# Two hi/lo pairs of matmul operands moved to other SBUF offsets in a float32r transformer kernel

## The reference

```python
def rms_norm(x, g):
    y = x * lax.rsqrt(jnp.mean(x * x, axis=-1, keepdims=True) + EPS)
    return y * g

def swiglu(h, w_gate_up, w_down):
    gate, up = jnp.split(h @ w_gate_up, 2, axis=-1)
    return (jax.nn.silu(gate) * up) @ w_down

# first block, layer i of 4
x = x + mixer_i(rms_norm(x, norm_mix_g[i]))
x = x + swiglu(rms_norm(x, norm_ffn_g[i]), ffn_w_gate_up[i], ffn_w_down[i])
# second block, layer i of 2
h = h + 0.5 * swiglu_ffn(rmsnorm(h, norm_ffn1[i]), w_ffn1_in[i], w_ffn1_out[i])
u = rmsnorm(h, norm_mix[i]) @ w_mix_in[i]
h = h + concat([ssd(u), attention(u)]) @ w_mix_out[i]
h = h + 0.5 * swiglu_ffn(rmsnorm(h, norm_ffn2[i]), w_ffn2_in[i], w_ffn2_out[i])
```

## Time and profile before

| | |
|---|---|
| median of 3 runs | 2777.88 us (2777.1 to 2781.78) |
| profiled execution | 2778.99 us |
| its span | 2777.2 us |
| mean granted TensorE clock | 0.973 of full |
| TensorE matmul busy | 2613.1 us, 94% |
| VectorE busy | 1834.5 us, 66% |
| ScalarE busy | 1266.6 us, 46% |
| moved by DMA | 433.01 MB, mean 156 GB/s |

### The profile page before, as it was taken

The page is one execution under the profiler, slowest core; times in us unless marked ns, Lnnn a source line. Parts: engine busy times, 40 slices in busy tenths (PEclk is TensorE's granted clock), DMA queues, the critical chain, the costliest instruction groups (busy, mean ns, idle before and its releaser), DMA issues.

```text
span 2777.2 us, 51613 instructions
## 1 busy us (share of the span) xinstructions
PE 2613.1 (94%) x21578; PEld 2531.9 (91%) x21578; DVE 1834.5 (66%) x2279; ACT 1266.6 (46%) x1489; POOL 292.3 (11%) x419
## 2 busy tenths in 40 slices
PE   7998854999999999999999999999999999999998
PEld 6998744999899988998999999999999999999998
DVE  3756778655666675554656656996656656986655
ACT  3434422533456565333434334665434334665433
POOL 7000481000300010000000000140000000140000
PEclk9999877999999999999999999999999999999999
DMA  4454101455567773553554554443554554443553
GB/s 172 179 182 166 31 1 30 155 195 181 157 178 160 159 167 106 185 183 120 183 189 167 197 181 161 155 148 143 183 184 168 195 183 159 155 153 140 183 182 121
DMA packets 77780, 433.01 MB, mean 156 GB/s; under 512 B 20224, under 2 KB 22784, under 8 KB 27728
## 3 DMA queue, kind: packets, MB, share of 16 engines
q1 hardware_dynamic: 58720, 410.25, 40.7%
q0 software_dynamic: 5888, 17.53, 5.2%
q10 hardware_dynamic: 13040, 3.34, 0.6%
HBM read 426.80 MB, written 3.24 MB: 155 GB/s over the span
## 4 chain that ended last, share of the span: by engine, by line
PE 86%; DVE 8%; ACT 3%; POOL 2%; issue 1%; DMA 1%; ACTq 0%; DVEq 0%; POOLq 0%
PE psum L1854 25%; PE psum L1856 25%; PE psum L1855 25%; PE psum L2143 1%; PE psum L1953 1%; PE psum L1887 1%; DVE w_lo L1309 1%; PE psum L2119 1%; PE psum L2131 1%; ACT w_hi L850 1%; DVE arena L1479 1%; DVE arena L1484 1%; PE psum L2122 1%; PE psum L1939 0%; DVE rstd L1334 0%
## 5 line engine op out<-in xcount | busy, mean ns | idle before, releaser
L1854 PE MATMUL psum<-h_hi,w_hi 128*128 128x256 f32 x4320 | 1219.7, 282 | 34.2 <-DVE h_lo L1347 15.5
L1856 PE MATMUL psum<-h_hi,w_lo 128*128 128x256 f32 x4320 | 1210.7, 280 | 0.0
L1855 PE MATMUL psum<-h_lo,w_hi 128*128 128x256 f32 x4320 | 1210.1, 280 | 0.0
L850 ACT ACTIVATE w_hi<-raw 128x2048 fp32r<-128x2048 f32 x387 | 740.2, 1914 | 908.7 <-PE psum L1856 908.7
L1309 DVE TENSOR_TENSOR w_lo<-raw,w_hi 128x2048 fp32r<-128x2048 f32 x387 | 886.1, 2290 | 388.2 <-ACT w_hi L850 388.0
L1854 PEld LDWEIGHTS psum<-h_hi,w_hi 128*128 128x128 f32 x4320 | 814.6, 189 | 45.8 <-issue 34.6
L1855 PEld LDWEIGHTS psum<-h_lo,w_hi 128*128 128x128 f32 x4320 | 815.6, 189 | 1.2 <-issue 1.0
L1856 PEld LDWEIGHTS psum<-h_hi,w_lo 128*128 128x128 f32 x4320 | 814.8, 189 | 0.0
L1854 PE MATMUL psum<-act_hi,w_hi 128*128 128x256 f32 x1536 | 430.0, 280 | 2.2 <-DVE w_lo L1309 1.5
L1856 PE MATMUL psum<-act_hi,w_lo 128*128 128x256 f32 x1536 | 429.3, 280 | 0.0
L1855 PE MATMUL psum<-act_lo,w_hi 128*128 128x256 f32 x1536 | 429.1, 279 | 0.0
(11 more groups left out here) (311 smaller groups left out, 2692.5 us busy)
## 6 DMA issues: line engine op xcount, KB each, us to landing
raw<-in_panels SPq DMA_DIRECT2D x387, 1024.0 KB, 4.8
arena<-bias_by_distance POOLq DMA_DIRECT2D x32, 384.0 KB, 7.8
x<-in_x SPq DMA_DIRECT2D x1, 1024.0 KB, 7.8
arena<-in_dft_sq ACTq DMA_DIRECT2D x2, 512.0 KB, 6.1
arena<-in_s_b SPq DMA_DIRECT2D x1, 1024.0 KB, 15.2
arena<-in_s_c SPq DMA_DIRECT2D x1, 1024.0 KB, 16.6
arena<-s_u POOLq DMA_DIRECT2D x1, 1024.0 KB, 5.1
arena<-arena POOLq DMA_DIRECT2D x32, 32.0 KB, 1.9
```

The source lines that it names most:

```text
L850: a.activation(w_hi[:, s, :], raw[:, s, :], ACT.Copy).then_inc(hi_ready, 1)
L1854: t.matmul(o, w[0], xin[0], start=start, stop=False, skip_group_check=True)
L1855: t.matmul(o, w[0], xin[1], start=False, stop=False, skip_group_check=True)
L1856: return t.matmul(o, w[1], xin[0], start=False, stop=stop, skip_group_check=True)
```

## The change

Only the order of declarations changes, and one unused tensor of 32 bytes is added. No instruction, loop, wait or DMA is added, removed or moved.

```diff
         gains = sb("gains", [P, A["gains"].shape[1]])
-        ones = sb("ones", [P, P])
-        zeros = sb("zeros", [P, P], F32R)
         eps = sb("eps", [P, 1])
         eps_head = sb("eps_head", [P, 1])
         warm = sb("warm", [P, 1])
         h_hi = sb("h_hi", [P, KT, S], F32R)
+        ones = sb("ones", [P, P])
         h_lo = sb("h_lo", [P, KT, S], F32R)
         rstd = sb("rstd", [P, S])
 
         hidden = sb("hidden", [P, 2, 2, 2, S])
         gate, act = hidden[:, 0], hidden[:, 1]
+        sb("act_hi_offset", [P, 8])
         act_hi = sb("act_hi", [P, 2, 2, S], F32R)
+        zeros = sb("zeros", [P, P], F32R)
         act_lo = sb("act_lo", [P, 2, 2, S], F32R)
         ident = sb("ident", [P, P])
```

## The result

The changed kernel takes 2790.24 us (median of 5 runs, 2789.46 to 2793.95) beside 2777.1 us before (5 runs, 2775.22 to 2781.78): slower by 0.5%, ratio 1.005 with a 95% interval of 1.0036 to 1.0065. This is the side of rival C, 1.2 us above the upper end of the range. The profiled execution took 2792.52 us, its span is 2790.7 us. Lines of the kernel have moved by one: `mm3` is now at 1855 to 1857.

What follows compares the result with a forecast made beforehand. TensorE's matmul pace, 117.8 ns in nearly all `mm3` triples, was taken to bound the kernel. All placement terms were 0 us on the profiled 2778.99 us; the forecast was the median, 2777.9 us, range 2757 to 2789 us.

Steps and rivals of the forecast that it cites:

- rival C: `act_hi`/`act_lo` reads meet weight loads, `down` at 120.0 ns: 10.1 us more, chance 0.09; with `project` 37.8 us, 0.03.
- `h_hi` and `h_lo`, 0 us: 12960 `project` matmuls and few of `project_tokens`: moves by 1024 and 512 bytes cost nothing, 0 us.
- `act_hi` and `act_lo`, 0 us: 4608 `down` matmuls: going from 64 to 96 past a multiple of 512 from `w_hi` costs 0 us.
- next rows: Moving tiles from `h` (multiple of 64 bytes) and mixer's `z` (60 past one): median 379 ns for both.
- the two bounds: For `down`'s 4608 matmuls: 20.3 us less at 113.3 ns, or 10.1 us more at 120.0 ns.
- A: The offset of 96 takes `down` to the fast pace: 20.3 us less, 2757.6 us, chance 0.08.
- the prediction's own sign of being wrong: A start between multiples of 64 bytes, or a distance the trace never varies, costs 1.2 ns or more.
- the strided row: Token panel of the dilated layer, stationary operand with every second element: 120.0 ns a matmul, 2.2 ns slower.
- rival D: Pace drawn anew at each stream's start: one SwiGLU 7.0 us less; one or two faster streams, chance 0.04.
- rival B: Distances to the weights set the pace, new ones good: 17184 matmuls gain 75.6 us, 2702.3 us, chance 0.05.
- The stream after S5: A stream of 384 matmuls already at 113.3 ns; losing that pace would cost 1.7 us.
- The rule of the two ports: TensorE reads moving operand and weights through independent ports, never waiting; so no placement can cost or win, supporting 0.

Runs made afterwards that it cites:

- experiment 2: The changed kernel without its unused 32-byte tensor, leaving moves by 512 and 1024 bytes: 2779.71 us beside 2781.6 before, ratio 0.999.
- experiment 3: Kernel before with 32 bytes ahead of `raw`, so every tensor lies 32 bytes higher at unchanged distances: 2778.36 us beside 2781.6, ratio 0.9984.
- Experiment 7: Kernel before with 32 bytes between `raw` and `w_hi`, changing only distances to `raw`: 2780.0 us beside 2777.76, ratio 1.0003.
- experiment 1: Kernel before with only 32 bytes added ahead of `act_hi`: 2789.66 us beside 2781.6, ratio 1.0026.
- 4: Kernel before with `h`/`act` at 96/128, 160/192, 256/320, 0/32 bytes modulo 512 from the weights: 2814.85, 2785.52, 2810.6, 2810.6 us.
- 5: Kernel before with `h` and `act` both at 192 bytes modulo 512 from the weights, both at 224, `act` alone at 192: 2720.63, 2804.66, 2775.71 us.
- Experiment 6: Kernel before with 32 bytes between `w_hi` and `w_lo`, putting only `w_hi` at 96 modulo 512 from `h` and `act`: 2790.56 us beside 2782.16.

## Why the prediction was wrong

**The bound** was read rightly. TensorE's pace sets the time, and what the offsets do to ScalarE and VectorE stays hidden: their idle time grew by what TensorE took longer.

**`h_hi` and `h_lo`, 0 us**: right. `project` kept 117.8 ns, and experiment 2 has the moves by 512 and 1024 alone at no price. Reading `project` against `down` in the trace of before was a fair test of multiples of 512.

**`act_hi` and `act_lo`, 0 us**: this is the step that failed. "I take 0, because the new places still start on a multiple of 32 bytes and every read is of adjacent elements, and because of the next rows." The start of a tile is not what counts (experiment 3); its distance to the weights is, and 96 is a slow one. The "next rows" compared matmuls whose starts lie 216 ns apart, too slow a pair to show a step of 2 ns, as the prediction noticed and didn't act on. With no row at the new distance, the two bounds should have stood beside each other with more than the 0.17 that A and C for `down` alone had together. The second half of the prediction's own sign of being wrong came true: a distance that its trace never varied has a price of 1.2 ns or more, here 2.2 ns. Rival C had the place, and its price of 10.1 us, taken from the strided row, is within 0.1 us of the 10.0 us measured in `down`. That the same 120.0 ns came out is no proof of one cause for both.

**The draw of the pace (rival D)** was seen and undervalued. "The place does not decide there; what is left is how the stream started" is right for 64, but the prediction let it speak against any effect of place (rival B). Both hold: the place decides which paces are open and how likely, the start picks one. "A stream passes from `h` to `act` without a change", the argument against A, fell too: with `act` at 192 the pace changes at each such passage in six of the eight SwiGLUs. "The runs lie within 4.7 us [...] and so show no such draw between executions" was a statement on three runs. Experiment 7 shows a SwiGLU that drew the fast pace, and experiment 3 a stream that left it at unchanged distances. Such a draw is a candidate for the spread from 2764 to 2788 us, but only one execution of each kernel was traced, so this stays an inference.

**The range** ended 1.2 us too low because it left 1.0 us of room above C. The stream after S5 lost 1.6 us (1.7 forecast in D), but other `project` panels gave more than that back, so what stands beside the 10.0 us of `down` in the two traces is mainly the 3.9 us of restarts, into which little can be read. Beside the larger sample of the kernel before the same step is worth 8.1 us (experiment 1), and 2777.9 + 8.1 = 2786.0 us would have lain inside the range. So the last 1.2 us say little; that there is a loss is clear in both comparisons (ratios from 1.0036 and from 1.0018 on).

**The rule of the two ports.** The prediction used the Trainium skill, "SBUF — State Buffer", section "Who interferes with whom" (TensorE reads moving operand and weights through two independent ports and waits on no one) as support for 0. The inference from it, that no placement can cost or win, is what the measurement decides against: the same instructions run at 113.3 to 120.0 ns by the distance of their operands. Whether it is the two kinds of reads that meet is argued below and not shown. For the best pace, the Trainium skill, "TensorE: Matmul & The Clock Gate", section "Back-to-back issue gap", has N/2.4 + 2.5 ns between isolated matmuls, 109.2 ns at 256 columns as an estimate from it, and says that in a stream of pairs of weight load and matmul both set the spacing. The best placement came to 113.3 ns, 4.1 above that estimate, and what the 4.1 are made of stays open.

**What is shown and what is not.** Shown: the pace depends on the distance, in steps of 32 bytes, between the `h` and `act` tiles and the weight buffers (experiments 1, 4, 5), not on the start alone (3), not on `raw` (7), not on multiples of 512 (2). That it is the loading of the next weights that meets the moving reads is argued: it is one of the accesses whose distance changes in experiment 1 and not in 3, it runs through all of a panel, as the steady pace does, and moving `w_hi` alone against the tiles redistributes the intervals (6). Its nearest rivals are ScalarE's and VectorE's writes into the same weight buffers, at the same distance from `act`. The trace of the changed kernel speaks against them. Both write for a part only of the `down` panel from 1116.59 to 1122.35:

```profile
1116.79 1.92 ACT L851 ACTIVATE w_hi<-raw 128x2048 fp32r<-128x2048 f32 x1 [3.22 <-PE psum L1857]
1119.41 2.29 DVE L1310 TENSOR_TENSOR w_lo<-raw,w_hi 128x2048 fp32r<-128x2048 f32 x1
```

Taking the intervals of the `down` panels in sixes (87 panels; one of the 88 holds a restart), a matmul takes 120.0 ns in the 93 sixes that lie wholly under such a write by ScalarE, 120.0 in the 237 under one by VectorE, and 120.0 in the 28 that touch neither. Experiment 6 limits the rest: the loads of `w_hi` at 96 alone don't give the slow pace, so it takes `w_lo` at 96, by itself or with `w_hi`, and which of the two is open. Open too: what in the memory makes some distances slow, and why the three prices don't add.

## What to carry to other kernels

When matmuls with a weight load each run back to back, read the distance of their starts and compare it between streams at the same clock; if two values appear, as 117.8 and 113.3 ns here, the placement of the operands is worth a sweep in steps of 32 bytes, and here it was worth 1.9% for 128 bytes of padding and an arena cut by 256. Sweep the distance between moving and stationary buffers, not the start of either. Don't take a quantity for free because no row varies it: put one small pad ahead of it and measure.

## What the runs showed of the hardware

- At full clock the same float32r matmul of 256 columns with its own weight load ran at 113.3, 117.4, 117.8 to 117.9, 118.3, 118.7 or 120.0 ns from start to start, by the distance of its moving tile from the weight buffers modulo 512 bytes.
- At one distance (64) two paces are stable over a SwiGLU's stream, 117.8 ns over some 189 us and 113.3 ns over 182 us; in 1 of 8 SwiGLUs of one run (experiment 7) the second was drawn, in the trace of before in none.
- In the slow `down` panels of the changed kernel the intervals repeat over six matmuls, 117, 125, 116, 123, 118 and 121 ns: the mean of 120.0 hides steps of up to 9 ns.
- In the slow `down` panels of the changed kernel the pace is 120.0 ns whether ScalarE or VectorE writes the weight buffers meanwhile or neither does (93, 237 and 28 groups of six intervals).
